# Gate rows by transfers from the modulation table instead of TensorE products in a two-layer diffusion transformer kernel

## What is computed

```python
for i in range(DEPTH):
    need_ctx = i < DEPTH - 1
    mod_l = (s_c @ ada_w[i] + ada_b[i])[:, None, :]
    mod_c = (s_cc @ ada_w[i] + ada_b[i])[None, None, :]
    sh1_l, sc1_l, g1_l, sh2_l, sc2_l, g2_l = jnp.split(mod_l, 6, axis=-1)
    sh1_c, sc1_c, g1_c, sh2_c, sc2_c, g2_c = jnp.split(mod_c, 6, axis=-1)
    h_l = rmsnorm(x_l, norm_g[i, 0]) * (1.0 + sc1_l) + sh1_l
    h_c = rmsnorm(x_c, norm_g[i, 0]) * (1.0 + sc1_c) + sh1_c
    if i % 2 == 0:
        out_c, out_l = even_mixer(h_c, h_l, ...)   # gated delta rule and latent attention
    else:
        out_c, out_l = odd_mixer(h_c, h_l, ...)    # neighbourhood attention, latent tokens
    x_l = x_l + g1_l * out_l
    ...                                            # the same for x_c with g1_c in layer 0
    f_l = rmsnorm(x_l, norm_g[i, 1]) * (1.0 + sc2_l) + sh2_l
    x_l = x_l + g2_l * ffn(f_l)                    # dense FFN in layer 0, 8 experts, top 2, in layer 1
```

## Time and profile before

| | |
|---|---|
| median of 3 runs | 2009.89 us (2006.91 to 2011.41) |
| profiled execution, first to last instruction (span) | 2010.4 us |
| PE (TensorE) busy | 1860.9 us, 93% |
| DVE (VectorE) busy | 659.6 us, 33% |
| ACT (ScalarE) busy | 488.8 us, 24% |
| POOL (GpSimd) busy | 426.2 us, 21% |
| memory traffic | 482.26 MB, mean 240 GB/s |
| granted TensorE clock, mean | 0.970 |

### The profile page before, as it was taken

One profiled execution on the slowest core, in us unless ns is written; L12 is line 12 of the kernel. 1 busy time (PEld: TensorE's weight loads), 2 busy tenths in 40 slices (PEclk: granted clock), 3 DMA queues, 4 the chain that ended last, 5 costly groups with the idle time before them and its releaser, 6 DMA issues.

```text
span 2010.4 us, 23259 instructions
## 1 busy us (share of the span) xinstructions
PE 1860.9 (93%) x9741; PEld 1120.2 (56%) x9742; DVE 659.6 (33%) x1198; ACT 488.8 (24%) x813; POOL 426.2 (21%) x240
## 2 busy tenths in 40 slices
PE   4999997989999989989979899999999999987896
PEld 1777645977777767878845444333433334332332
DVE  4951865645000023471064332111321112211223
ACT  3323355544221121242153210110111011111111
POOL 1431563631334433435641000000000000000000
PEclk8998999999999999989989999999999999998998
DMA  9345000132455551227235799999989998999996
GB/s 352 116 175 182 6 0 1 43 126 84 169 173 187 188 189 60 104 85 142 89 74 199 282 416 409 400 389 413 383 332 401 398 392 316 412 410 413 412 413 260
DMA packets 149869, 482.26 MB, mean 240 GB/s; under 512 B 26388, under 2 KB 51397, under 8 KB 135413
## 3 DMA queue, kind: packets, MB, share of 16 engines
q1 hardware_dynamic: 149296, 479.85, 62.7%
q10 hardware_dynamic: 453, 0.65, 0.1%
HBM read 479.43 MB, written 1.05 MB: 239 GB/s over the span
## 4 chain that ended last, share of the span: by engine, by line
PE 65%; DMA 4%; SPq 4%; DVE 4%; issue 1%; ACT 1%; POOL 1%; DVEq 0%; ACTq 0%
PE PS L2667 21%; PE PS L2684 10%; PE PS L2110 8%; PE PS L2111 8%; PE PS L2112 8%; SPq L637 3%; DMA BIG<-in_od_exp_wu 2%; PE PS L2638 1%; PE PS L2628 1%; PE PS L2583 1%; PE PS L2658 1%; DMA BIG<-in_od_exp_wg 1%; PE PS L2089 1%; SPq L634 1%; DVE X L1706 1%
## 5 line engine op out<-in xcount | busy, mean ns | idle before, releaser
L2667 PE MATMUL PS<-BIG,QB 128*64 128x448 f32 x1424 | 304.1, 553 | 22.7 <-DMA BIG<-in_od_exp_wu 13.5
L2684 PE MATMUL PS<-BIG,ZS 128*64 128x512 f32 x966 | 218.0, 593 | 2.5 <-ACT ZS L1303 2.5
L2667 PEld LDWEIGHTS PS<-BIG,QB 128*64 128x64 f32 x1424 | 109.6, 140 | 194.0 <-issue 192.4
L699 POOL TENSOR_TENSOR BIG_parts<-BIG,QB_parts 128x2048 fp32r<-128x2048 f32 x33 | 152.7, 4629 | 267.5 <-ACT QB_parts L876 267.5
L2667 PE MATMUL PS<-BIG,HB 128*64 128x448 f32 x944 | 200.8, 547 | 8.9 <-issue 8.9
L699 POOL TENSOR_TENSOR BIG_parts<-BIG,BIG_parts 128x2048 fp32r<-128x2048 f32 (+1 forms) x28 | 125.3, 4475 | 215.6 <-ACT BIG_parts L876 215.6
L2684 PEld LDWEIGHTS PS<-BIG,ZS 128*64 128x64 f32 x966 | 70.7, 137 | 135.1 <-issue 134.3
L2111 PE MATMUL PS<-HB_parts,QB_parts 128*128 128x512 f32 (+1 forms) x384 | 143.5, 374 | 0.0
L2667 PEld LDWEIGHTS PS<-BIG,HB 128*64 128x64 f32 x944 | 72.4, 138 | 121.1 <-issue 119.8
L1303 ACT ACTIVATE ZS<-PS 128x896 f32<-128x896 f32 x32 | 29.4, 918 | 416.4 <-PE PS L2658 416.4
L2111 PE MATMUL PS<-BIG_parts,BIG_parts 128*128 128x512 f32 (+1 forms) x304 | 115.8, 381 | 0.0
(11 more groups left out here) (395 smaller groups left out, 3088.6 us busy)
## 6 DMA issues: line engine op xcount, KB each, us to landing
BIG<-in_od_exp_wg SPq DMA_DIRECT2D x63, 1792.0 KB, 17.7
BIG<-in_od_exp_wu SPq DMA_DIRECT2D x56, 1792.0 KB, 13.9
BIG<-in_od_exp_wd SPq DMA_DIRECT2D x55, 1792.0 KB, 18.0
BIG<-in_ada_w SPq DMA_DIRECT2D x24, 2048.0 KB, 7.9
QB<-in_od_exp_wd SPq DMA_DIRECT2D x9, 1792.0 KB, 13.5
QB<-in_od_exp_wu SPq DMA_DIRECT2D x8, 1792.0 KB, 14.5
BIG<-in_od_w_qkv SPq DMA_DIRECT2D x6, 2048.0 KB, 11.1
BIG<-in_ev_ffn_wg SPq DMA_DIRECT2D x11, 1024.0 KB, 8.8
```

The costliest lines, as they stand in the source:

```text
L699: pool.tensor_tensor(r12(w), w, r12(high), ALU.subtract).then_inc(split_l, 1)
L2667: last = mm(PS[at:at + 64, bank, 0:GROUP], XGS[x][:, 4 * part + k, r0:r0 + 64], wgu[u][:, k, GROUP * c:GROUP * c + GROUP], start=(part + k ...
L2684: last = mm(PS[64 * n:64 * n + 64, bank, :], HET[:, s % 2, k, r0:r0 + 64], half[:, a, :], start=(k == 0), stop=(k == 6))
```

## The change

The twelve products, their 12 copies and the semaphores `gb_mm` and `gb_ready` go. SyncE sends the rows instead: for each gate and each half of 512 columns one transfer whose source is one row of `MOD`, repeated 128 times, and whose target is all 128 partitions; twelve in all, counted by `gates_in`. A new buffer `XT` holds `GB0`; `GA1`, in a part of `HB` that is free, holds layer 1's `g1`. The scratch for transfers that GpSimd would issue is set to 1024, which makes the room for `XT`.

```diff
+        XT = sb("XT", [P, 3840], parts=[(0, 3840)])
...
-        GB0 = AR[:, 0:2 * D].rearrange("p (r n) -> p r n", r=2)
+        GB0 = XT[:, 0:2 * D].rearrange("p (r n) -> p r n", r=2)
+        GA1 = HB[:, 2048:2048 + D]
...
+            def load_gate(to, g, c0, r):
+
+                for c in range(2):
+                    q = 32 * (c0 + c) + r
+                    row = MOD[q:q + 1, g:g + 1, :].to_broadcast([1, P, 512])
+                    sp.dma_start(to[:, 512 * c:512 * c + 512], row).then_inc(gates_in, 16)
...
+                if i == first["out0"]:
+                    sp.wait_ge(tok_mm, 8)
+                    sp.wait_ge(mod_rows, 2)
+                    for r in range(2):
+                        load_gate(GB0[:, r, :], 1, 0, r)
+                if i == first["up3"]:
+                    sp.wait_ge(mod_rows, 3)
+                    sp.wait_ge(out_mm, 2 * NT)
+                    for r in range(2):
+                        load_gate(GB[:, r, :], 2, 2, r)
...
+            begin(sp, None, "natt")
+            sp.wait_ge(mod_rows, 6)
+            load_gate(GA1, 1, 0, 0)
+            load_gate(GE, 2, 2, 0)
 
             for i in range(NBIAS, NP):
                 load_bias(i)
...
-            dve.wait_ge(gb_mm, 1)
             dve.wait_ge(go_sum, NT)
-            for r in range(2):
-                for c in range(2):
-                    last = dve.tensor_copy(GB0[:, r, 512 * c:512 * c + 512], PS[:, 4 + 2 * r + c, :])
-            last.then_inc(gb_ready, 1)
...
-                dve.wait_ge(gb_ready, 1 if stage == "out0" else 4)
+                dve.wait_ge(gates_in, 64 if stage == "out0" else 192)
...
-                    gate, tmp = (GB0[:, t // 2, cols], OT) if stage == "out0" else (GB[:, t // 2, cols], ZS)
+                    gate, tmp = (GB0[:, t // 2, cols], OT) if stage == "out0" else (GA1[:, cols], ZS)
...
+            dve.wait_ge(gates_in, 128)
             for t in range(NT):
...
             begin(pe, "pe", "gout")
-            gate_rows(1, 0, 2)
...
-            pe.wait_ge(gb_ready, 1)
...
-            for r, c, bank in FFN_GATES[0:3]:
-                last = gate_row(2, 2, r, c, bank)
-            last.then_inc(gb_mm, 1)
             for f in range(2, FF // P):
                 pe.wait_ge(up_ev, f - 1)
                 up_products(f, 0, T).then_inc(up_mm, 1)
-                if f == 2:
-                    pe.wait_ge(gb_ready, 2)
-                    gate_row(2, 2, *FFN_GATES[3]).then_inc(gb_mm, 1)
...
             begin(pe, "pe", "out1")
-            gate_rows(1, 0, 1)
-            gate_rows(2, 2, 1, 6)
...
-    nc = bacc.Bacc("TRN2", target_bir_lowering=False, num_devices=1)
+    nc = bacc.Bacc("TRN2", target_bir_lowering=False, num_devices=1, dynamic_dma_scratch_size=1024)
```

More of the change, by code:

```diff
@@ L238, in build @@
         N1_BANK = (4, 6, 5, 5)
-        FFN_GATES = ((0, 0, 5), (0, 1, 6), (1, 0, 7), (1, 1, 5))
         DT = AR[:, 11264:11264 + 2 * 512].rearrange("p (a n) -> p a n", a=2)
@@ L474, in build @@
         sm_tr, sm_cols = sem("small_transposed"), sem("small_columns")
-        mod_rows, ada_tr, gb_mm = sem("mod_rows"), sem("ada_transposed"), sem("gate_rows_mm")
+        mod_rows, ada_tr, gates_in = sem("mod_rows"), sem("ada_transposed"), sem("gates_in")
         norm_sd, norm_rstd, xn_ready, norm_tr, norm_ev = (sem(n) for n in (
@@ L512, in pair @@
             return 4 * s + 2 * d + i + 1
-        gb_ready, go_tr, go_ev, go_sd, go_n = (sem(n) for n in ("gate_rows_ready", "o_transposed", "o_columns", "o_sd",
+        go_tr, go_ev, go_sd, go_n = (sem(n) for n in ("o_transposed", "o_columns", "o_sd",
                                                                 "o_gated"))
@@ L1124, in _ @@
             act.nop().then_inc(done["act"], 1)
[L1126 to L1130, removed]
-                    for c in range(2):
-                        last = act.activation(to[:, r, 512 * c:512 * c + 512], PS[:, 4 + 2 * r + c, :], ACT.Copy)
-                last.then_inc(gb_ready, 1)
-                act.wait_ge(gb_ready, k + 1)
             begin(act, "act", "out0")
@@ L1168, in _ @@
                 act.nop().then_inc(done["act"], 1)
[L1170 to L1175, removed]
             for f in range(FF // P):
@@ L1254, in _ @@
             attention(N_PAIRS, NM, PC, PCT, 2, DH ** -0.5)
[L1256 to L1260, removed]
+            begin(act, "act", "out1")
             act.activation(SS[:, 20:21], EPSC[:, 0:1], ACT.Sqrt)
@@ L1280, in _ @@
                 act.activation(X[:, 2 + i, :], X[:, i, :], ACT.Copy, scale=SS[:, 16 + i:17 + i]).then_inc(xn_ready, 1)
-            act.wait_ge(gb_ready, 5)
             act.wait_ge(xn_ready, 14)
@@ L2469, in ffn_turned @@
                 pe.wait_ge(xn_ready, 4 + i + 1)
-                if i == 0:
-                    pe.wait_ge(gb_ready, 1)
                 if i >= 2:
@@ L2586, in _ @@
             for t in range(2):
-                pe.wait_ge(gb_ready, 4 + t)
                 pe.wait_ge(out_ev, 2 * NT + 2 + t + 1)
```

3 lines of the change are left out of this document (removed).

## The result

| | before | after |
|---|---|---|
| median of the runs, us | 2009.5 (2006.9 to 2011.4, 4 runs) | 2059.0 (2058.5 to 2060.4, 4 runs) |
| ratio, with 95% interval | | 1.024 [1.023, 1.0255] |
| span of the profiled execution, us | 2010.4 | 2057.7 |
| TensorE busy, us | 1860.9 | 1848.5 |

A forecast was written before the change was run, and what follows sets the result against it. TensorE, busy 93% of the span, was taken as the bound, with SyncE's queue releasing at the attention's start. Gains of 10.4 us against delays of 35.3, 1.6 and 40.8 gave +67.3: 2077.2 us, range 2018 to 2115.

The forecast's parts named there:

- G: SyncE's queue: how long a set of four row transfers (1.05 MB) keeps it; 40.8 us taken, 2.5 from below.
- First set: Before out0: four row transfers in SyncE's empty gap after 196.26 us, even 40.8 us hidden; cost 0.
- Second set: In "up", ahead of the fourth chunk of FFN weights: chunk late by G, TensorE stalls 35.3 us, plus 1.6 for the clock.
- The slack: In "up": the fourth chunk's low part is ready at 549.25, TensorE takes it up at 554.78; 5.5 us.
- the slower restart: In "up" after the stall: TensorE's granted clock is 0.57 at first, costing 1.6 us.
- Third set: At the attention's start, between out1 weights and bias blocks: no slack, so the whole attention waits 40.8 us.
- Gains: TensorE time from removed gate products: 3.0 us in "gout", 3.7 in "up", 3.7 in "out1"; together 10.4 us.
- The sum: Whole kernel: -10.4 + 35.3 + 1.6 + 40.8 = +67.3 us, added to the median 2009.9 for 2077.2 us.
- The full rate: Rival 1, all sets: G about 2.5 us, sum -7.9, 2002.0 us, faster; chance 0.12.
- later transfers overtake a slow set: Variant of the full-rate rival, SyncE's queue: G large but nobody waits; -10, 1999 us; chance 0.03.

The follow-up runs named there:

- The probes: The changed kernel plus single 256 KB transfers from various source partitions in SyncE's empty stretch behind the first set; 2060.0 us (one run).
- the second kernel: The changed kernel with only the third set moved, behind the four last bias blocks; 2037.3 us, ratio to before 1.0138.
- the two kernels that leave room for it: Second and third sets moved, plus either third-set rows sent through sixteen partitions (1999.2 us) or GE transfers waiting for attention steps (1999.6 us).
- the two that stop: The changed kernel with the third set moved behind the bias blocks (2037.3 us), and with the second set moved as well (2006.1 us).

## Why the prediction was right, point by point

- **What a set takes (G).** Forecast 40.8 us from 411 / 16 = 25.7 GB/s. The probes give 26 GB/s from one partition, and the first set took 40.4 us. The mechanism (rows read from one partition hold up SyncE's queue) and its size were right, and with them the sign. The reason given (one partition feeds what one DMA engine moves) was not quite the thing: one row keeps all sixteen engines busy, and the limit is on the side that is read, since two rows of one side share 26 GB/s and two of different sides get 51. That the size came out all the same is luck in part: these 51 GB/s took the time of two engines, so one engine and one side move about the same here.
- **First set, 0:** right. TensorE's times show no step that belongs to it.
- **Second set, G - 5.5 = 35.3 and 1.6 for the clock:** measured 31.8. The step that was off is that the whole of G was added to the chunk's landing. From the order ahead of the set to the landing of the chunk it was 542.64 - 529.15 = 13.5 us before and 569.13 - 520.24 = 48.9 after: 35.4 more, since the first row transfer already moved beside the 2 MB of the order ahead. The slack came out as forecast: 35.4 - 5.5 = 29.9, by which TensorE's first product with the chunk is later, and 1.9 more in the products behind it for the slower restart, forecast 1.6 (granted clock 0.50 in 575 to 580).
- **Third set, 40.8:** measured 27.8, the largest error. The same step failed more: from the issue of the out1 weights to the landing of the bias block it was 1020.47 - 1006.61 = 13.9 us before and 1070.50 - 1028.88 = 41.6 after, 27.7 more. "The queue is already busy then" was read as a reason for no slack; it meant that the row packets start beside 2 MB of weights whose landing takes 9.1 us anyway, and only then hold up the rest. With all four rows from one side the delay was 32.1 us (36.99 - 4.94), 8.7 less than a whole set; the other 4.3 are what the second side gives at the changeover, which the forecast put at nothing.
- **Gains:** 3.0, 3.7 and 3.7 were forecast for "gout", "up" and "out1"; 2.2, 3.5 and 3.4 came. In "gout" VectorE begins to scale where the forecast had it, but takes 4.71 us and not 4.29, and the last four transposes take 0.66 us behind it. The 1.6 us of granted clock behind "gout" are in no term.
- **The sum:** +67.3 forecast, +47.3 between the spans, 20.0 less. Of these 5.1 are in "up", 13.0 in the attention, 1.6 the granted clock before "gout" (it differs by 0.7 to 5.2 us between before and the changed kernels' traces), 1.6 the granted clock behind "gout" and 0.7 a piece between "up" and the attention; against them the gains came 1.3 short, and 0.7 were lost behind "out1". The term of the sum that was mis-sized is the third set's, 40.8 for 27.8, and behind it the second's.
- **A slip.** Of 2.5 and 40.8 us for a set the prediction says that both ends stay in the range; the time that goes with 2.5, 2002 us, is not in its 2018 to 2115.
- **The rivals.** The full rate was excluded by the probes for one row, and shown for a spread source. That later transfers overtake a slow set is excluded by the chain. Nothing of instruction packets was in the prediction. In the change they do no harm, since TensorE stands still anyway while set 3 runs; they came out only when the transfers were moved.

What stays open: no record says for which engine an instruction packet is. That the late one was TensorE's is concluded from TensorE stopping at the same instruction twice, starting again within 3 us of the packet (in the second kernel it came in the microsecond from 1073, and TensorE went on at 1075.97), and not stopping in the two kernels that leave room for it. The count agrees: in the two that stop, the packet comes after 10433 of TensorE's own records (products and weight loads) and TensorE has stopped there; in the changed kernels that do not stop it comes after 10201 to 10360.

## What to carry to other kernels

Before a row is spread by DMA, ask from how many partitions it is read: 256 KB took 11 us from one partition, 6.7 from two on different sides and 2.6 from sixteen, so a first hop to sixteen partitions pays for itself at once (a set of four rows in 12.6 us in place of some 38). A transfer that is slow at its source costs most by its place: all that stands behind it in the same queue is late by most of its length (35.4 and 27.7 us of 40), so put it where that queue has nothing due, and count as delay only what goes beyond the work already under way. And where TensorE stops in the middle of equal instructions with no releaser, look for the packets of the instruction queue and for what holds the DMA engines just then.

## What was not expected of the hardware

- A row read from one partition into 128 keeps all sixteen DMA engines busy (share 0.84 to 0.91 in most windows) for 26 to 28 GB/s; the same bytes from two partitions in one transfer take a share of 0.13, the time of two engines.
- Instruction packets come late beside such rows. The first of the attention came at 1042 us in place of 1027 to 1031, and TensorE stood still for 3.7 us (5.6 in the other kernel), with products at half clock behind it (5.1 us lost in all, 7.4 in the other).
- Two row transfers from different sides, one behind the other in one queue, hardly overlap: 18.8 us against 20.9 from the same side (one measurement each).
